# A paced top-k, an opening by passes, and three norm sums from fp32r halves in a two-block transformer kernel

## The chip, the cores and the metric

The kernel runs on one core of a Trainium2 chip. A core has a matrix engine (TensorE, PE in the profile; its weight load is PEld), a vector engine (VectorE, DVE), a scalar engine (ScalarE, ACT), GpSimd (POOL) and a sync engine (SyncE, SP), each with an instruction queue of its own; they wait for each other by semaphores. DMA queues bring data from memory, and all tiles live in on-chip memory (SBUF) or in the eight accumulator banks of PE (PSUM, "bank" in the profile). The metric is the device time of one execution in microseconds, lower is better.

## The reference, cut to what matters

Two transformer blocks run one after the other on 512 tokens of width 1024, all in float32.

```python
def first_block(x, ...):
    h = rmsnorm(x, ln1)                       # norm n1
    z = h @ w_in                              # pool, GLA and forgetting-attention (FoX) inputs
    mix = concat(y_pool, y_gla, y_fox)
    x = x + mix @ w_o
    h = rmsnorm(x, ln2)                       # norm n2
    gate, up = split(h @ w_gu)
    x = x + (silu(gate) * up) @ w_down
    return rmsnorm(x, ln_f)                   # norm n3 (its gain is folded on)

def second_block(x, ...):
    h = rmsnorm_2(x, norm_g)                  # norm n3f works on x as well
    q_lat, c_kv, k_rope, z_a, q_b, k_b, v_b, z_b, q_idx, k_idx, w_idx, gate_a, gate_b = split(h @ w_in)
    y_a = mla_attention(...) * silu(z_a)      # 8 heads, softmax over chunk-causal keys
    # index scores: relu(q_idx k_idx) weighted over 8 index heads; top 128 keys of each query
    _, idx = lax.top_k(score, 128)
    y_b = dsa_attention(... gathered by idx ...) * silu(z_b)
    merged = sigmoid(gate_a) * (y_a @ w_o_a) + sigmoid(gate_b) * (y_b @ w_o_b)
    return rmsnorm_2(x + merged @ w_out, final_g)
```

## The kernel before, in words

**Products.** Activations are held transposed: width on the 128 partitions, 512 tokens along the row. A dense product is made of 128x128 weight tiles, 1296 of them in all, in units of eight. Weights and activations are each split into a high and a low fp32r half, so that one tile costs three matmuls into the same bank: high x high (L1454), low activation (L1456) and low weight (L1458). `WS` holds a unit of weights as loaded, `WH` and `WL` its halves; ACT makes WH (L1638, 128x1024) and either DVE (L1856) or POOL (L2234, in quarters) makes WL. `HH` and `HL` are the halves of the activation x: ACT makes HH (L1646 in the opening, L1767 later), DVE HL (L1866, L2072).

**Order.** A planner in Python writes one list of steps with `do(...)`; each of the five engine programs walks that list and issues its part of each step. So the order on every engine is fixed when the program is built. A `product` yields after every two tiles; `weave(main, side, per)` runs the attention (`main`) and pulls steps of the side products (`side`) in between at a rate of `per`. `behind` is a list of lesser work. At every yield of a product `go_behind` adds `now["per"]` to a debt and issues one piece of that work for each whole unit of it. From the attention of the second block on, the list holds the top-k: `top(i)` gives 16 rounds for each of the query blocks i=3, 2, 1, and a round is one MAX8 (L2145) and one MATCH_REPLACE8 with its load (L2147) on DVE, 512 or 384 or 256 wide.

**Rings.** Banks and buffers are handed out by rings, each with the event that frees its next member: `d_ring` (banks 0, 1) for products, `s_ring` (2, 3) for logits, `t_ring` (4, 5) for turned shares and the sums, `y_ring` (6, 7) for attention outputs, `tmp_ring` (two 128x512 buffers) for temporaries of ACT and DVE.

**Attention.** For a unit (head pair, head, query block i) PE computes logits (L1562, L1563), DVE their row maximum (L2031), ACT the exponentials (L1736), DVE the inverse of the sum (RECIPROCAL, L2046), ACT multiplies (the share, L1741), PE turns the result by products with the identity (L1577), ACT moves it out of the bank (L1749) and PE mixes it with the values (L1586). I write (pair, n) for the n-th unit of a pair of MLA heads, counted through both heads, as in "the turn of unit (0,3)".

**Norms.** A norm needs the sum over the width of the squares. They are accumulated in a 128x512 fp32 tile `acc`; `column_sums` then does one fp32 product with a tile of ones (L1496, two records in the trace), and ACT computes exp(-0.5 ln(.)) of the bank (L1654, L1657) into `Rb` or `Rf`. There are six such sums: n1, n2, n3, n3f and those of the two latents of MLA. The sum of n2 stands after six of the eight tiles of the first gate product of the FFN (`gate0`), n3 inside the index query product `qi0`, n3f behind `qi1`; next on PE is there the latent product `ckv0`.

**The opening.** `start` issues on SP: vecs, the first half of the first weight unit (`WS[:, 0, 0:512]`), X chunk 0, its second half, X1, W1, X2, X3, W2 and so on. Until the first halves are ready PE runs 14 products of ones (28 records). Then the first three products (`firsts`: three columns of w_in) run together: for each chunk k of the input the three products have one tile each.

**The rope of the key** (`keys`, DVE L2122, L2123, L2125) takes both buffers of `tmp_ring` and gives them back when its last instruction ends; that is event `rope("end")`. It stands in the list right ahead of the sum of n3f (`norm_first`).

## Time and profile before

| | us |
|---|---|
| median of 3 runs | 1049.0 (1048.12 to 1049.06) |
| the profiled execution: its time | 1049.3 |
| its span in the trace | 1047.5 |
| PE busy | 1030.2 (98%) |
| PEld busy | 832.4 (79%) |
| DVE busy | 603.8 (58%) |
| ACT busy | 443.9 (42%) |
| POOL busy | 320.5 (31%) |
| granted clock of PE, mean | 0.997 |

The page gives busy time by engine, the span in 40 slices and the costliest groups of instructions. A timeline row gives the start, the duration, the engine and the instruction; in square brackets stands how long the engine was idle ahead of it and what ended that. Matmuls overlap in the records: a 128x512 fp32r matmul is drawn 0.39 us long, and the next begins 0.227 us after it (232.80, 233.02, 233.25 and so on in an undisturbed stretch), so the pace of PE is the distance of starts. What PE loses at a place is the distance of two starts less what that pair of instructions takes elsewhere, which is a little more than the idle time in brackets.

### The profile page before, as it was taken

The page shows a single profiled execution, that of the slowest core. Times are in us where ns is not written, and L with a number is a line of the kernel's source. Part 1 is how long each engine was busy: PE and PEld are TensorE (multiplying, and loading weights), DVE is VectorE, ACT ScalarE, POOL GpSimd, SP SyncE. Part 2 cuts the span into 40 slices and gives each one's busy share as a digit, 9 for nine tenths or more (in the row PEclk, how much of TensorE's full clock was granted, in tenths as well). Part 3 has the DMA queues.
Part 4 walks back from the last instruction along what each step waited for, and adds up shares of the span by engine and source line. Part 5 has one row for each costly group of instructions (what it writes and reads, how often), then busy time and mean ns, then how long its engine had stood idle before and what let it go on. Part 6 is the DMA issues. An engine that isn't in the chain of part 4 may idle for free.

```text
span 1047.5 us, 13717 instructions
## 1 busy us (share of the span) xinstructions
PE 1030.2 (98%) x5126; PEld 832.4 (79%) x5126; DVE 603.8 (58%) x1087; ACT 443.9 (42%) x785; POOL 320.5 (31%) x374
## 2 busy tenths in 40 slices
PE   9999999999999999999999999989999999999997
PEld 7887877778888888888888878767887777788886
DVE  5875657575444432444457657888656666335544
ACT  6432656554232221233242346445755554323233
POOL 1344632440110000110113347333336666521101
PEclk9999999999999999999999999999999999999999
DMA  8222233123323322323322335211322323222312
GB/s 287 92 71 86 82 91 94 62 77 104 100 84 104 115 92 90 101 81 101 101 101 89 126 115 190 81 61 45 98 67 85 116 88 109 84 98 95 106 61 81
DMA packets 34898, 102.39 MB, mean 98 GB/s; under 512 B 4608, under 2 KB 8128, under 8 KB 34832
## 3 DMA queue, kind: packets, MB, share of 16 engines
q1 hardware_dynamic: 34560, 101.25, 29.7%
q8 instruction: 41, 0.67, 0.3%
q10 hardware_dynamic: 272, 0.26, 0.1%
q14 instruction: 25, 0.20, 0.1%
HBM read 93.40 MB, written 4.74 MB: 94 GB/s over the span
## 4 chain that ended last, share of the span: by engine, by line
PE 85%; DVE 8%; ACT 3%; issue 2%; DMA 1%; POOL 0%; SPq 0%; DVEq 0%; ACTq 0%; POOLq 0%
PE bank L1454 23%; PE bank L1458 23%; PE bank L1456 23%; PE bank L1586 3%; PE bank L1577 2%; PE bank L1477 1%; DVE score L2147 1%; PE bank L1478 1%; PE bank L1479 1%; DVE m L2145 1%; PE bank L1562 1%; DVE acc L1875 1%; ACT WH L1638 1%; DMA X<-xT 1%; PE bank L1496 1%
## 5 line engine op out<-in xcount | busy, mean ns | idle before, releaser
L1454 PE MATMUL bank<-HH,WH 128*128 128x512 f32 x800 | 322.7, 403 | 0.9 <-DVE HL L1866 0.6
L1458 PE MATMUL bank<-HH,WL 128*128 128x512 f32 x800 | 312.9, 391 | 0.0
L1456 PE MATMUL bank<-HL,WH 128*128 128x512 f32 x800 | 312.5, 391 | 0.0
L2234 POOL TENSOR_TENSOR WL<-WS,WH 128x256 fp32r<-128x256 f32 x256 | 203.5, 795 | 255.6 <-ACT WH L1638 239.6
L1638 ACT ACTIVATE WH<-WS 128x1024 fp32r<-128x1024 f32 x160 | 166.3, 1047 | 41.6 <-PE bank L1458 40.2
L1454 PEld LDWEIGHTS bank<-HH,WH 128*128 128x128 f32 x800 | 151.0, 189 | 38.5 <-issue 5.8
L1458 PEld LDWEIGHTS bank<-HH,WL 128*128 128x128 f32 x800 | 150.4, 188 | 32.3
L1456 PEld LDWEIGHTS bank<-HL,WH 128*128 128x128 f32 x800 | 150.9, 189 | 29.4 <-issue 1.4
L1856 DVE TENSOR_TENSOR WL<-WS,WH 128x1024 fp32r<-128x1024 f32 x96 | 125.1, 1308 | 30.8 <-ACT WH L1638 30.8
L2275 POOL TENSOR_TENSOR fa<-fa,fg 128x512 f32<-128x512 f32 x22 | 28.3, 1286 | 271.6 <-DVE fa L2087 271.6
L1454 PE MATMUL bank<-GH,WH 128*128 128x512 f32 x176 | 68.5, 389 | 0.0
L1456 PE MATMUL bank<-GL,WH 128*128 128x512 f32 x176 | 68.5, 389 | 0.0
L1458 PE MATMUL bank<-GH,WL 128*128 128x512 f32 x176 | 68.5, 389 | 0.0
L2067 DVE TENSOR_TENSOR X<-X,bank 128x512 f32<-128x512 f32 x39 | 26.7, 685 | 66.5 <-PE bank L1458 66.4
L1775 ACT ACTIVATE GH<-fa 128x512 fp32r<-128x512 f32 x22 | 13.9, 632 | 114.6 <-POOL fa L2275 114.6
L1650 ACT ACTIVATE sq<-X 128x512 f32<-128x512 f32 x31 | 19.5, 629 | 75.4 <-DVE X L2067 75.3
L1477 PE MATMUL bank<-WH,HH 128*128 128x256 f32 x160 | 47.3, 296 | 0.1
L1749 ACT ACTIVATE PT<-bank 128x128 f32<-128x128 f32 (+1 forms) x96 | 41.1, 428 | 14.0 <-PE bank L1577 13.7
L1479 PE MATMUL bank<-WH,HL 128*128 128x256 f32 x160 | 45.2, 283 | 0.0
L1478 PE MATMUL bank<-WL,HH 128*128 128x256 f32 x160 | 45.2, 283 | 0.0
L2089 DVE TENSOR_TENSOR GL<-fa,GH 128x512 fp32r<-128x512 f32 x22 | 15.2, 692 | 47.1 <-ACT GH L1775 47.1
L1771 ACT ACTIVATE fs<-fg 128x512 f32<-128x512 f32 x22 | 13.9, 632 | 59.3 <-DVE fg L2078 59.3
(326 smaller groups left out, 1710.7 us busy)
## 6 DMA issues: line engine op xcount, KB each, us to landing
WS<-wall SPq DMA_DIRECT2D x161, 512.0 KB, 3.4
scratch<-rows SPq DMA_DIRECT2D x8, 320.0 KB, 5.4
X<-xT SPq DMA_DIRECT2D x8, 256.0 KB, 6.8
b_t<-scratch SPq DMA_DIRECT2D x8, 256.0 KB, 3.6
outT<-X SPq DMA_DIRECT2D x7, 256.0 KB, 2.3
b_m<-b_m SPq DMA_DIRECT2D x11, 128.0 KB, 2.3
f_s<-f_s SPq DMA_DIRECT2D x8, 128.0 KB
f_m<-f_m SPq DMA_DIRECT2D x8, 128.0 KB
```

What stands on the lines that cost most here:

```text
L1454: e.matmul(b[:, :], wh, xh[:, at_k, :], start=k == 0, stop=False)
L1456: e.matmul(b[:, :], wh, xl[:, at_k, :], start=False, stop=False)
L1458: m = e.matmul(b[:, :], wl, xh[:, at_k, :], start=False, stop=k == n - 1)
L1477: e.matmul(b[:, 0:256], xh[:, k, cs], wh, start=k == 0, stop=False)
L1478: e.matmul(b[:, 0:256], xh[:, k, cs], wl, start=False, stop=False)
L1479: m = e.matmul(b[:, 0:256], xl[:, k, cs], wh, start=False, stop=k == NK - 1)
L1586: m = e.matmul(b[64 * hl:64 * hl + 64, 128 * kb:512], v[:, kb, hd * 64:hd * 64 + 64], s["pt"][:, at_pt + 128 * kb:at_pt + 512], start=kb = ...
L1638: e.activation(WH[:, u % NW, :], WS[:, u % NST, :], ACT.Copy).then_inc(*w_hi.tick(u))
L1749: e.activation(dst, s["b"][:, 0:128 * i + 128].rearrange("p (a n) -> p a n", n=128), ACT.Copy).then_inc(*moved.tick(s["u"]))
L1856: e.tensor_tensor(WL[:, u % NW, :], WS[:, u % NST, :], f32(WH[:, u % NW, :]), ALU.subtract).then_inc(*w_low_v.tick(u))
L2234: e.tensor_tensor(WL[:, u % NW, cs], WS[:, u % NST, cs], f32(WH[:, u % NW, cs]), ALU.subtract).then_inc(*tick(w_low_g, u if c == 3 else (u ...
L2275: e.tensor_tensor(a[:, :], a[:, :], fg[jj % 3][:, :], ALU.mult).then_inc(*tick(gate_up, jj))
```

## The change

It has five parts.

1. **Opening.** X chunk 0 is issued by ACT, ahead of its table load, not by SP. On SP, X1 then stands in front of the second half of the first weights, X2 in front of W1, and X4 in front of W2. PE runs 10 products of ones, not 14. ACT and DVE halve the second part of the first weights after X1 rather than after X0. For each k, PE runs the three high products, then the three with the low activation, then the three with the low weight (`mm_firsts`).
2. **Sums from halves.** For n2, n3 and n3f ACT copies `acc` to an fp32r tile in one `tmp_ring` buffer (the high half), DVE subtracts it from `acc` into the other (the low half), and PE multiplies both with `ones_r`, two fp32r matmuls in the place of one fp32 matmul. POOL makes `ones_r` once.
3. **The place of n2.** The sum follows all eight tiles of `gate0`, not six.
4. **za1.** The gate product of MLA pair 1 (six tiles and two, 8 in all) opens the side products instead of following uq3; the first query product uq0 takes its bank from `t_ring`.
5. **Pacing.** `go_behind` no longer issues rounds (`now["per"]` is 0); `paced` wraps the attention and issues one round each time that .25 per attention step and .37 per product tile add up to 1. Ahead of `step_c` (the turn) of MLA there is one more yield to the side products.

```diff
@@ column_sums
+            halved = name in ("n2", "n3", "n3f")
+            if halved:
+                (m1, _, free1), (m2, _, free2) = tmp_ring.take(), tmp_ring.take()
+                do("sums_halves", name=name, a=a, ready=ready, hi=tmp_r[m1], lo=tmp_r[m2], free1=free1, free2=free2)
             i, b, free = t_ring.take()
-            do("sums", name=name, a=a, ready=ready, b=b, free=free)
+            if halved:
+                do("sums", name=name, halves=(tmp_r[m1], tmp_r[m2]), b=b, free=free)
+                tmp_ring.give(m1, sums(name))
+                tmp_ring.give(m2, sums(name))
+            else:
+                do("sums", name=name, a=a, halves=None, ready=ready, b=b, free=free)
@@ planner, the opening
-        do("split_first", half=0)
         for c in range(NK):
             do("halve_x", c=c)
-            if c == 0:
-                do("split_first", half=1)
+            if c < 2:
+                do("split_first", half=c)
...
-            for (name, _, _, _), (t, _), b in zip(firsts, tiles, early):
-                do("mm", name=name, tiles=[(t, k)], n=NK, x="h1", x0=0, b=b, free=None)
+            do("mm_firsts", names=[f[0] for f in firsts], tiles=[t for t, _ in tiles], k=k, b=early)
@@ the attention's order
                         if to_c:
+                            if to_c[0]["a"] == "mla":
+                                yield
                             step_c()
@@ gate_out, and the loop of the FFN
+                if jj == 0:
+                    ffn_norm()
                 do("ffn_gate", half=half, j=j, jj=jj, b=b)
...
-                if jj == 0:
-                    for _ in range(3):
-                        next(gen)
-                    ffn_norm()
@@ mla_products
-                                   + cols(96 * hd + 64, 16), "lq", 3, q_out(hd, hl))
-            if p:
+                                   + cols(96 * hd + 64, 16), "lq", 3, q_out(hd, hl),
+                                   ring=t_ring if hd == 0 else d_ring)
+            if p > 1:
                 yield from z_products("za", P_ZA, p)
...
         def mla_side():
+            yield from z_products("za", P_ZA, 1)
             yield from mla_products(1)
...
+        def paced(main, per_tile, per_step):
+            due, seen = 0.0, len(steps)
+            for _ in main:
+                yield
+                due += per_step + per_tile * sum(len(s["tiles"]) if kind == "mm" else 2 * (kind == "mm_tok")
+                                                 for kind, s in steps[seen:])
+                seen = len(steps)
+                while due >= 1:
+                    due -= 1
+                    step_behind()
...
-        now["per"] = 1.5
+        now["per"] = 0.0
@@ SP, the start
-                    for c in range(NK):
+                    for c in range(1, NK):
                         e.dma_start(X[:, c, :], xT[:, c, :]).then_inc(*x_in[c].tick())
-                        if c == 0:
+                        if c == 1:
                             e.dma_start(WS[:, 0, 512:1024], wall[0, :, 512:1024]).then_inc(*w_in[0].tick(0))
-                        elif c in (1, 3):
-                            load((c + 1) // 2)
+                        elif c in (2, 4):
+                            load(c // 2)
@@ PE
-                    for _ in range(14):
+                    for _ in range(10):
...
+                elif kind == "mm_firsts":
+                    k = s["k"]
+                    for t, b in zip(s["tiles"], s["b"]):
+                        q.wait_ge(hi(("h1", k)), w_hi("first" if t < 4 else t // UT))
+                        e.matmul(b[:, :], weights(t)[0], HH[:, k, :], start=k == 0, stop=False)
+                    for t, b in zip(s["tiles"], s["b"]):
+                        q.wait_ge(low(("h1", k)))
+                        e.matmul(b[:, :], weights(t)[0], HL[:, k, :], start=False, stop=False)
+                    for name, t, b in zip(s["names"], s["tiles"], s["b"]):
+                        q.wait_ge(w_low_v("first") if t < 4 else split_low(t // UT))
+                        m = e.matmul(b[:, :], weights(t)[1], HH[:, k, :], start=False, stop=k == NK - 1)
...
                 elif kind == "sums":
-                    q.wait_ge(s["ready"], s["free"], fill("ones"))
-                    e.matmul(s["b"][:, :], ones[:, :], s["a"][:, :], start=True, stop=True).then_inc(
-                        *sums.tick(s["name"]))
+                    if s["halves"]:
+                        hi_sum, lo_sum = s["halves"]
+                        q.wait_ge(norm_a(s["name"] + " hi"), s["free"], fill("ones_r"))
+                        e.matmul(s["b"][:, :], ones_r[:, :], hi_sum[:, :], start=True, stop=False)
+                        q.wait_ge(norm_v(s["name"] + " lo"))
+                        e.matmul(s["b"][:, :], ones_r[:, :], lo_sum[:, :], start=False, stop=True).then_inc(
+                            *sums.tick(s["name"]))
@@ ACT
+                    e.dma_start(X[:, 0, :], xT[:, 0, :]).then_inc(*x_in[0].tick())
                     e.preload_act_table_set(LN_EXP)
...
+                elif kind == "sums_halves":
+                    q.wait_ge(s["ready"], s["free1"])
+                    e.activation(s["hi"][:, :], s["a"][:, :], ACT.Copy).then_inc(*norm_a.tick(s["name"] + " hi"))
@@ DVE
+                elif kind == "sums_halves":
+                    q.wait_ge(norm_a(s["name"] + " hi"), s["free2"])
+                    e.tensor_tensor(s["lo"][:, :], s["a"][:, :], f32(s["hi"][:, :]), ALU.subtract).then_inc(
+                        *norm_v.tick(s["name"] + " lo"))
```

The opening on PE, before, from the products of ones on; the waits of a row stand in brackets by the name of the semaphore (hi and low: the halves of X; w_hi and w_low_v: those of the weights):

```order
L1443 MATMUL bank<-ones 128x128 x13
L1454 MATMUL bank<-HH,WH 128x512 [waits hi,w_hi]
L1456 MATMUL bank<-HL,WH 128x512 [waits low]
L1458 MATMUL bank<-HH,WL 128x512 [waits w_low_v]
L1454 MATMUL bank<-HH,WH 128x512
L1456 MATMUL bank<-HL,WH 128x512
L1458 MATMUL bank<-HH,WL 128x512
...
L1454 MATMUL bank<-HH,WH 128x512 [waits hi]
L1456 MATMUL bank<-HL,WH 128x512 [waits low]
L1458 MATMUL bank<-HH,WL 128x512
```

And now:

```order
L1468 MATMUL bank<-ones 128x128 x9
L1487 MATMUL bank<-HH,WH 128x512 [waits w_hi,hi]
L1487 MATMUL bank<-HH,WH 128x512 x2
L1490 MATMUL bank<-HL,WH 128x512 [waits low]
L1490 MATMUL bank<-HL,WH 128x512 x2
L1493 MATMUL bank<-HH,WL 128x512 [waits w_low_v]
L1493 MATMUL bank<-HH,WL 128x512 x2
L1487 MATMUL bank<-HH,WH 128x512 [waits hi]
L1487 MATMUL bank<-HH,WH 128x512 [waits w_hi]
L1487 MATMUL bank<-HH,WH 128x512
L1490 MATMUL bank<-HL,WH 128x512 [waits low]
```

What stood as a triple of high, low activation and low weight for each tile stands now as three passes, and each pass has the wait that it needs.

The sum of n3f on PE, before and now. The row ahead of it is the last tile of `qi1`, the one behind it the first of `ckv0`:

```order
L1458 MATMUL bank<-HH,WL 128x512
L1496 MATMUL bank<-acc_66,ones 128x512 [waits norm_a,total_g]
L1454 MATMUL bank<-HH,WH 128x512 [waits w_low_v,out_v]
L1456 MATMUL bank<-HL,WH 128x512
L1458 MATMUL bank<-HH,WL 128x512
```

```order
L1478 MATMUL bank<-HH,WL 128x512
L1533 MATMUL bank<-tmp_r,ones_r 128x512 [waits norm_a]
L1535 MATMUL bank<-tmp_r,ones_r 128x512 [waits norm_v]
L1476 MATMUL bank<-HH,WH 128x512 [waits w_low_v,out_v]
L1477 MATMUL bank<-HL,WH 128x512
L1478 MATMUL bank<-HH,WL 128x512
```

ACT around the same place, before and now (L1697 is the copy into the high half, L1842 the halves of the index queries, L1701 and L1704 the norm, L1682 the weight splits):

```order
L1638 ACTIVATE WH<-WS 128x1024 [waits dense,w_in2]
L1790 ACTIVATE i_kk<-i_s 32x512 [waits out_v]
L1791 ACTIVATE i_kk<-i_s 32x512
L1795 ACTIVATE i_qh<-i_q 128x512 [waits out_v] x2
L1654 ACTIVATE Rf<-bank,eps 128x512 [waits sums]
L1657 ACTIVATE Rf<-Rf 128x512 [waits norm_a]
L1638 ACTIVATE WH<-WS 128x1024 [waits dense,w_in0]
L1638 ACTIVATE WH<-WS 128x1024 [waits dense,w_in1]
```

```order
L1682 ACTIVATE WH<-WS 128x1024 [waits dense,w_in2]
L1837 ACTIVATE i_kk<-i_s 32x512 [waits out_v]
L1838 ACTIVATE i_kk<-i_s 32x512
L1842 ACTIVATE i_qh<-i_q 128x512 [waits out_v] x2
L1697 ACTIVATE tmp_r<-acc_67 128x512 [waits rope,total_g]
L1701 ACTIVATE Rf<-bank,eps 128x512 [waits sums]
L1704 ACTIVATE Rf<-Rf 128x512 [waits norm_a]
L1682 ACTIVATE WH<-WS 128x1024 [waits dense,w_in0]
```

DVE there, now: the rope of the key takes L2173 to L2176, and L1925 makes the low half:

```order
L2168 TENSOR_TENSOR i_ql<-i_q,i_qh 128x512 [waits istack_a] x2
L2173 TENSOR_TENSOR tmp_72<-i_s,RT 32x512 [waits sums,rope_in,out_v]
L2174 TENSOR_TENSOR tmp_71<-i_s,RT 32x512
L2176 TENSOR_TENSOR a_k_199<-tmp_72,tmp_71 32x512 [waits rope]
L1925 TENSOR_TENSOR tmp_r<-acc_67,tmp_r 128x512 [waits rope,norm_a]
```

The sum waits for `norm_a` (the copy) and `norm_v` (the subtraction), where it waited for the total; the copy waits for `rope` as well, which is the end of the row L2176 of DVE. On ACT the copy stands in front of the two weight splits.

DVE from the RECIPROCAL (the inverse sum) of the MLA unit (0,1) to that of (0,3), before (L2145 and L2147 are a round of the top-k, L1891 and L1895 the gate product za1):

```order
L2046 RECIPROCAL small<-small 128x1 [waits exps]
...
L2145 MAX m_74<-score 128x8 [waits topk]
L2147 MATCH_REPLACE score<-m_74,score 128x512 [waits topk]
L2145 MAX m_74<-score 128x8 [waits topk]
L2147 MATCH_REPLACE score<-m_74,score 128x512 [waits topk]
L2145 MAX m_74<-score 128x8 [waits topk]
L2147 MATCH_REPLACE score<-m_74,score 128x512 [waits topk]
L2046 RECIPROCAL small<-small 128x1 [waits exps]
...
L1891 SCALAR_TENSOR_TENSOR zb_212<-bank,Rb 128x512 [waits dense]
L1895 SCALAR_TENSOR_TENSOR zb_212<-tmp_71,zb_212 128x512 [waits tanh]
L2145 MAX m_74<-score 128x8 [waits topk]
...
L2046 RECIPROCAL small<-small 128x1 [waits exps]
```

And now (rounds are L2196 and L2198, L2223 writes the queries of the next pair):

```order
L2097 RECIPROCAL small<-small 128x1 [waits exps]
L2082 TENSOR_REDUCE small<-bank 128x1 [waits share_v,logits]
L2223 SCALAR_TENSOR_TENSOR a_q_197<-bank,RQ 128x512 [waits dense]
L2196 MAX m_77<-score 128x8 [waits topk]
L2198 MATCH_REPLACE score<-m_77,score 128x512 [waits topk]
L2097 RECIPROCAL small<-small 128x1 [waits exps]
L2082 TENSOR_REDUCE small<-bank 128x1 [waits share_v,logits]
L2223 SCALAR_TENSOR_TENSOR a_q_198<-bank,RQ 128x512 [waits dense]
L2196 MAX m_77<-score 128x8 [waits topk]
L2198 MATCH_REPLACE score<-m_77,score 128x512 [waits topk]
L2196 MAX m_77<-score 128x8 [waits topk]
...
L2097 RECIPROCAL small<-small 128x1 [waits exps]
```

Five rounds and the gate (za1) stood between the two in the order before; three rounds and the queries of the next pair stand there now. Ahead of the RECIPROCAL of (0,3) there were nine rounds in all, now there are six.

## Rows read from the trace of the kernel before

**Rows 1.** The page: busy times, and the chain that ended last.

```profile
PE 1030.2 (98%) x5126; PEld 832.4 (79%) x5126; DVE 603.8 (58%) x1087; ACT 443.9 (42%) x785; POOL 320.5 (31%) x374
...
PE 85%; DVE 8%; ACT 3%; issue 2%; DMA 1%; POOL 0%; SPq 0%; DVEq 0%; ACTq 0%; POOLq 0%
```

**Rows 2.** PE's timeline, 0 to 16 us (start, length, instruction, [idle before]).

```profile
1.00 5.98 PE L1443 MATMUL bank<-ones 128*128 128x128 f32 x28 [1.00 <-POOL ones L2215]
...
14.26 0.50 PE L1454 MATMUL bank<-HH,WH 128*128 128x512 f32 x1 [0.31 <-DVE HL L1866]
```

**Rows 3.** The same timeline, ACT and then DVE.

```profile
10.01 0.72 ACT L1646 ACTIVATE HH<-X,V 128x512 fp32r<-128x512 f32 x1 [1.15 <-DMA X<-xT]
10.64 1.04 ACT L1638 ACTIVATE WH<-WS 128x1024 fp32r<-128x1024 f32 x1
...
13.46 0.75 DVE L1866 SCALAR_TENSOR_TENSOR HL<-X,V,HH 128x512 fp32r<-128x512 f32 x1
```

**Rows 4.** Timeline, 233 to 240 us (the sum of n2): PE, ACT, DVE.

```profile
234.73 1.12 PE L1496 MATMUL bank<-acc,ones 128*128 128x512 f32 x2 [0.41 <-DVE acc L1875]
...
235.93 0.40 PE L1456 MATMUL bank<-HL,WH 128*128 128x512 f32 x1
...
234.47 1.04 ACT L1638 ACTIVATE WH<-WS 128x1024 fp32r<-128x1024 f32 x1
...
234.60 0.75 DVE L2072 SCALAR_TENSOR_TENSOR HL<-X,V,HH 128x512 fp32r<-128x512 f32 x1
235.54 1.23 DVE L1856 TENSOR_TENSOR WL<-WS,WH 128x1024 fp32r<-128x1024 f32 x1 [0.19 <-ACT WH L1638]
```

**Rows 5.** Groups of instructions of the page: busy us, mean ns of one.

```profile
L1775 ACT ACTIVATE GH<-fa 128x512 fp32r<-128x512 f32 x22 | 13.9, 632 | 114.6 <-POOL fa L2275 114.6
...
L2089 DVE TENSOR_TENSOR GL<-fa,GH 128x512 fp32r<-128x512 f32 x22 | 15.2, 692 | 47.1 <-ACT GH L1775 47.1
```

**Rows 6.** Timeline, 593 to 599 us (the sum of n3): DVE, PE.

```profile
594.29 3.44 DVE L1856 TENSOR_TENSOR WL<-WS,WH 128x1024 fp32r<-128x1024 f32 x2
...
597.50 1.02 PE L1496 MATMUL bank<-acc,ones 128*128 128x512 f32 x2
...
598.60 0.40 PE L1456 MATMUL bank<-HL,WH 128*128 128x512 f32 x1
```

**Rows 7.** Timeline, 606 to 617 us (the sum of n3f): PE, DVE.

```profile
607.93 1.02 PE L1496 MATMUL bank<-acc,ones 128*128 128x512 f32 x2
...
609.21 0.39 PE L1456 MATMUL bank<-HL,WH 128*128 128x512 f32 x1
...
609.57 1.29 DVE L2117 TENSOR_TENSOR i_ql<-i_q,i_qh 128x512 fp32r<-128x512 f32 x2
...
612.33 1.11 DVE L2125 TENSOR_TENSOR a_k<-tmp,tmp 32x512 f32<-32x512 f32 x1
```

**Rows 8.** PE at 685 us, and a stretch: length, PE busy, PEclk 0.50.

```profile
685.37 0.84 PE L1577 MATMUL bank<-ident,Pc 128*128 128x128 f32 x4 [2.73 <-ACT Pc L1741]
...
685.70:689.10 3.40, 3.40 (x11) 2.63 (x9) 3.30 (x9) 1.72 (x5) 0.00 (x0) 0.50 0.45 159
```

**Rows 9.** Ten us of the attention: length, then busy PE, PEld, DVE.

```profile
665.00:675.00 10.00, 10.00 (x47) 7.73 (x46) 9.70 (x24) 3.54 (x10) 3.18 (x6) 1.00 0.20 72
```

**Rows 10.** Timeline of PE, 657 to 727 us: the other waits.

```profile
660.36 0.50 PE L1454 MATMUL bank<-LQH,WH 128*128 128x512 f32 x1 [1.09 <-DVE a_k L2169]
...
704.29 0.65 PE L1586 MATMUL bank<-PT,a_v 128*64 128x512 f32 x2 [0.41 <-ACT PT L1749]
...
724.38 0.44 PE L1577 MATMUL bank<-ident,Pc 128*128 128x128 f32 x2 [0.97 <-ACT Pc L1741]
```

**Rows 11.** Timeline of DVE, 680 to 709 us.

```profile
680.89 0.69 DVE L1895 SCALAR_TENSOR_TENSOR zb<-tmp,zb 128x512 f32<-128x512 f32 x1 [1.04 <-ACT tmp L1660]
...
684.41 0.15 DVE L2046 RECIPROCAL small<-small 128x1 f32<-128x1 f32 x1
...
707.65 0.69 DVE L2172 SCALAR_TENSOR_TENSOR a_q<-bank,RQ 128x512 f32<-128x512 f32 x1 [2.12 <-PE bank L1458]
```

27 lines of the change are left out of this document (17 added, 10 removed).

## The prediction

> **What bounds the kernel now.** Read the busy times first [rows 1]: PE is busy for 1030.2 of 1047.5 us, and the chain that ended last runs over PE for 85% of the span. So a faster ACT, DVE or POOL is worth nothing in itself. What can be won are the places where PE stands still, the products of ones ahead of the first real one, and the fp32 sums. What can be lost is any new place where PE must wait. I therefore went through PE's timeline for rows in which the distance of two starts is more than the usual 0.227 us, and then read the timelines of ACT and DVE at each of these places, to see which instruction is the late one and what stands ahead of it. The largest lot, 7.9 us, lies between 660 and 727 us, in the MLA attention. Its worst row is the turn of unit (0,3), with 2.73 us of idle [rows 8].
>
> The sum is made against the profiled execution (1049.3 us). The median is 0.3 lower, and the changes are taken over to it unaltered.
>
> **Opening: -1.35 us.** PE waits last at 14.26 us, for the low half of X3 [rows 2]. From there on it runs without a gap. So what counts is when HL3 is ready and how much of the work of k=3 is done by then. HL3 is made at 13.46 to 14.21; its engine was held up by the weight split, that waits for ACT's WH at 10.64, which stood behind HH2, for which ACT waited 1.15 us for the DMA of X2 [rows 3]. With X2 issued ahead of the weights, HH2 comes earlier; W1 now lands behind X2, an estimate of 10.0 us since the two together end where X2 ended before (10.01). WH then starts at 10.0 instead of 10.64, so everything behind it is 0.65 earlier. Then the passes: three high products of k=3, 3 x 0.227 = 0.68 us, need only HH3 and run inside the wait. Together 1.35. The cover is that PE, with fewer waits, doesn't meet HL4 or the next WL late; HL4 follows HL3 on DVE by an addition and itself, some 1.4 us [rows 3, 5], and a k costs PE 9 x 0.227 = 2.05 us, so it doesn't. Bounds: -0.7 (the passes alone) to -2.0 (a further wait, at 11.57 [rows 2], goes as well). The products of ones took 5.98 us for 14, so ten end near 5.3, before PE is fed; that costs nothing unless the clock comes later (below).
>
> **n2: +0.65 us.** Before, the sum stood after six tiles at 234.73, and the second matmul of the next tile at 235.93, 1.20 us later, where a plain one is 0.227 later [rows 4]. Two short matmuls would take 0.45, so 0.5 is to be won where nothing waits. But now all eight tiles come first, and the last one waits for HL7 (234.60 + 0.75 = 235.35) [rows 4]. The copy stands on ACT behind the WH split (to 235.51) and takes 0.63 [rows 4, 5], so to 236.15. The subtraction (0.69 [rows 5]) stands on DVE behind the WL split, which ends at 236.77 [rows 4]: ready 237.46. The short pair follows, and the first product of `up0` starts at about 237.75, not 237.09 (the six matmuls from 235.93 less one, at 0.227). That is +0.65; between +0.2 (the subtraction slips ahead) and +0.9. The norm `Rb` comes later too, but the bank of `gate0` is wanted only six us on, so that hides.
>
> **n3: +0.33 us.** The sum cost 598.60 - 597.50 = 1.10, less 0.227. Now the subtraction stands on DVE behind two WL splits that end at 594.29 + 3.44 = 597.73 [rows 6], so it is ready at 598.42; the next tile starts at 598.70, not 598.37. Between 0 and +0.5.
>
> **n3f: +7.7 us, the term that decides.** Before, this sum took `acc` as it was: 607.93, and the tile behind it was under way by 609.21 [rows 7], at pace from 608.98. Now the copy needs both buffers of `tmp_ring`, and these are held by the rope of the key, which comes one step before it in the list. The copy's row says so: it waits for `rope`. On DVE the rope is the last of a row of work: the index queries' low halves at 609.57 (two of them), then three instructions of 32x512, the last from 612.33 to 613.44 [rows 7]. None of it waits for PE any longer, and none gets faster, save that last instruction: it took 1.11 us beside a WL split on POOL that won't have begun, where a plain one takes 0.69 [rows 5], so it may end at 613.0. Copy 0.63, subtraction 0.69 [rows 5], with some 0.1 for the signals: 614.4 to 614.9. Behind the two short matmuls `ckv0` starts at 614.7 to 615.2 instead of 608.98: +5.7, between +5.5 and +6.2. Behind the waiting matmul on PE's queue stands all of the rest; behind the waiting copy on ACT stand the norm and two weight splits, which come some 5 us later than before; their units are wanted on PE over 10 us after the wait, so that hides. Then the clock: after the idle of 2.73 us at 682.6 PE had clock 0.50 for 3.4 us, and its matmuls came every 0.43 us [rows 8], so some 1.6 us were lost; waits of 1.09 and 0.97 us [rows 10] cost none. A wait of over five us is past the 2.73 that did it; I take 2.0, between 1.5 and 2.7. The sum is 7.7.
>
> A rule of the Trainium skill stands behind the purpose of this part. FP8 and Floating Point Precision, section TensorE Precision Notes, says that a true fp32 product takes four passes through the array. The rows agree (about 0.9 for the sum and 0.227 for an fp32r matmul). By that rule alone the three sums would give back some 1.5 us together, where I have +8.7 from the waits.
>
> **MLA attention: -4.4 us.** What PE loses here before, each as the distance of starts beyond the pace: 1.5 at 660.36, where uq1 waits for the bank of uk0 [rows 10], 2.9 at 685.37 and 1.6 by the clock behind it [rows 8], 1.14 at 724.38, 0.35 at 704.29 [rows 10] and 0.38 in one place more: 7.9 in all. The first goes, since uq0 takes its bank from another ring and six tiles of za1 stand in front, less 0.3 for the next wait of that kind. The second is the turn of unit (0,3): its RECIPROCAL is late, at 684.41, behind a wait of DVE for the gate za1 (1.04 us at 680.89) and nine rounds [rows 11] of about 1.5 us (two of them fill the time from the gate's end, 681.5, to 684.41). In the new order six rounds stand there, and the gate is done long before. But PE comes earlier too: DVE is busy for 9.70 of 10 us [rows 9], so what it has less to do ahead of that unit, PE doesn't find waiting for it. I count the share ready at 682.4 and PE there at 681.3: 1.1 is left. And the rounds that are not ahead of (0,3) are ahead of a later one. In the old order DVE had caught up at 705 us (2.12 us of idle at 707.65 [rows 11]); with PE over 4 us earlier it has not, and the turn of (2,2) waits 2.05 by my count (ready 708.85, PE 706.8). So 7.9 - 0.3 - 1.1 - 2.05 = 4.4. Bounds: 3 (the wait of 2 us costs clock as well) to 6.5 (rounds are spread well enough for one of the two to hide).
>
> A rule of the skill bears on DVE here. SBUF, section on the two separate sides, says that a DVE instruction with two SBUF inputs and a GpSimd instruction that reads SBUF exclude one another. This trace agrees: 3.44 us for two WL splits beside POOL [rows 6], 1.23 for one [rows 4]. Where the rounds move beside POOL's splits, DVE could lose more than I count; no row here has a price for the rounds.
>
> **Sum.** -1.35 + 0.65 + 0.33 + 7.7 - 4.4 = +2.9, so 1051.9 us.
>
> **The rivals.**
> - *The attention gives back nearly all.* If the paced rounds remove all 7.9 and the opening 2.0, with the rest as above: 1049.0 - 7.9 - 2.0 + 8.7 = 1047.8. For it speaks that rounds come one at a time and each unit has some slack; against it DVE's 9.70 of 10 [rows 9], for pacing moves work on DVE and takes none away. 0.22.
> - *DVE is the bound and the pacing gives nothing.* Each us won at (0,3) is lost at the next turn; only the 1.5 of the start stays: 1049.0 - 1.35 + 8.7 - 1.5 = 1054.9. 0.15.
> - *The other side: the n3f sum does not hold PE.* If the copy finds its buffers free, or the rope ends long before 613, the three sums cost +0.5 in all: 1049.0 - 1.35 + 0.5 - 4.4 = 1043.7. It decides for faster from the point where n3f costs under 2.6 us, clock included; `ckv0` starts 1.7 after the rope's end, so the rope would have to be over by 609.9, which [rows 7] speak against. The copy's row names `rope`, so 0.06.
> - *The clock.* The fall of the clock comes twice more, behind the 2 us wait at (2,2) and in the opening with its shorter warm-up, at 1.6 each [rows 8]: 1051.9 + 3.2 = 1055.1. Against it, waits of 1.09 and 0.97 cost nothing [rows 10]. 0.12.
> - The forecast, each term within its bounds: 0.45, from 1050.2 to 1053.6.
>
> **How the numbers follow.** This kernel's runs differ by about 0.1%; 0.2%, 2.1 us, is what can be told from no change. Faster (under 1046.9): the rope rival and a quarter of the first, 0.12. Same (to 1051.1): three quarters of the first and a quarter of the forecast's own range, 0.28. Slower: 0.60. The range takes in most of each case but the one on the rope: 1046.8 to 1055.2.
>
> **What would show it.** In the trace after, PE's row of the first short sum matmul of n3f has an idle of over 5 us in brackets, put down to ACT or DVE, and PEclk shows 0.50 behind it; the copy on ACT starts where the rope's last instruction ends. The opening's last wait of PE stands before 14 us and is shorter, and PE's sum of n1 comes 1.3 earlier. `up0` starts 2 us after HL7 is done. In the attention the turn of (0,3) waits about 1 us at full clock, and that of (2,2) about 2. The prediction is wrong if the n3f row has no such idle, if DVE shows idle time between 665 and 705, or if the clock falls in the opening.

## The result, and the profile after

| | before | changed |
|---|---|---|
| median | 1049.01 us (12 runs, 1047.92 to 1049.36) | 1051.68 us (12 runs, 1050.33 to 1052.56) |
| ratio of the changed kernel to the one before | | 1.0026, 95% interval 1.0019 to 1.0034 |
| the profiled execution: time, span | 1049.3, 1047.5 | 1051.26, 1049.4 |
| granted clock of PE, mean | 0.997 | 0.994 |

The changed kernel is slower by 0.26%: 2.7 us by the medians, 1.96 by the two profiled executions. The page of the changed kernel (compare [rows 1]):

```profile
PE 1028.1 (98%) x5118; PEld 831.6 (79%) x5118; DVE 604.2 (58%) x1090; ACT 445.8 (42%) x788; POOL 319.3 (30%) x375
```

PE is busy 2.1 us less in a span that is 1.9 us longer, so PE stands still for 4 us more. As before, the time is made of the places where it waits. I compare the two timelines of PE at points that both kernels pass in the same order:

| PE reaches | before | changed | difference | of this part |
|---|---|---|---|---|
| the sum of n1 | 22.55 | 20.63 | -1.92 | opening -1.92 |
| the first tile of `up0`, behind n2 | 237.09 | 235.89 | -1.20 | n2 +0.72 |
| the last matmul of `qi1`, behind n3 | 607.70 | 606.86 | -0.84 | n3 +0.36 |
| the sum of the first latent | 628.35 | 635.08 | +6.73 | n3f +7.57 |
| the last mix of the attention (L1586, L1629) | 902.28 | 904.13 | +1.85 | attention -4.88 |
| its last instruction | 1040.29 | 1042.15 | +1.86 | 0 |

**Opening.** ACT, then DVE, then PE; L1690 is ACT's HH, L1682 its WH, L1913 DVE's HL (compare [rows 2, 3]):

```profile
8.17 0.71 ACT L1690 ACTIVATE HH<-X,V 128x512 fp32r<-128x512 f32 x1
9.35 1.06 ACT L1682 ACTIVATE WH<-WS 128x1024 fp32r<-128x1024 f32 x1 [0.47 <-DMA WS<-wall]
...
12.19 0.74 DVE L1913 SCALAR_TENSOR_TENSOR HL<-X,V,HH 128x512 fp32r<-128x512 f32 x1
...
12.19 0.84 PE L1487 MATMUL bank<-HH,WH 128*128 128x512 f32 x3
12.99 0.97 PE L1490 MATMUL bank<-HL,WH 128*128 128x512 f32 x3
```

HH2 starts at 8.17, where it was 10.01, and WH1 at 9.35, where it was 10.64. HL3 is at 12.19 instead of 13.46. PE's waits at 11.57 and 14.26 are gone; its passes follow each other with only some 0.25 us lost between 12.19 and 13.80, where two passes of three matmuls take 0.80 and 0.81 instead of 0.68. The figure of -1.92 is that of one pair of executions. In the runs below the sum of n1 stands between 22.13 and 23.54 us with the old opening and between 19.95 and 21.14 with the new one, so the medians of the runs are the better measure of this part.

**n2.** PE and DVE (compare [rows 4]):

```profile
233.53 0.50 PE L1476 MATMUL bank<-HH,WH 128*128 128x512 f32 x1 [0.41 <-DVE HL L2123]
...
234.33 0.40 PE L1533 MATMUL bank<-tmp_r,ones_r 128*128 128x512 f32 x1
235.55 0.50 PE L1535 MATMUL bank<-tmp_r,ones_r 128*128 128x512 f32 x1 [0.82 <-DVE tmp_r L1925]
...
233.66 1.23 DVE L1903 TENSOR_TENSOR WL<-WS,WH 128x1024 fp32r<-128x1024 f32 x1 [0.19 <-ACT WH L1682]
234.81 0.69 DVE L1925 TENSOR_TENSOR tmp_r<-acc,tmp_r 128x512 fp32r<-128x512 f32 x1
```

The eighth tile waits 0.41 us for HL7, and the second short matmul 0.82 us for the subtraction, which stands behind the weight split at 233.66. `up0` begins at 235.89, 1.56 us after the first short matmul.

**n3** (compare [rows 6]):

```profile
597.20 0.50 PE L1535 MATMUL bank<-tmp_r,ones_r 128*128 128x512 f32 x1 [0.50 <-DVE tmp_r L1925]
...
593.09 3.45 DVE L1903 TENSOR_TENSOR WL<-WS,WH 128x1024 fp32r<-128x1024 f32 x2
596.47 0.68 DVE L1925 TENSOR_TENSOR tmp_r<-acc,tmp_r 128x512 fp32r<-128x512 f32 x1
```

The same with two weight splits, 0.50 us of wait.

**n3f.** PE, ACT, DVE (compare [rows 7, 8]):

```profile
606.86 0.39 PE L1478 MATMUL bank<-HH,WL 128*128 128x512 f32 x1
612.95 0.80 PE L1533 MATMUL bank<-tmp_r,ones_r 128*128 128x512 f32 x1 [5.70 <-ACT tmp_r L1697]
613.67 0.80 PE L1535 MATMUL bank<-tmp_r,ones_r 128*128 128x512 f32 x1
...
612.26 0.63 ACT L1697 ACTIVATE tmp_r<-acc 128x512 fp32r<-128x512 f32 x1 [3.62 <-DVE a_k L2176]
...
611.49 0.68 DVE L2176 TENSOR_TENSOR a_k<-tmp,tmp 32x512 f32<-32x512 f32 x1
612.92 0.69 DVE L1925 TENSOR_TENSOR tmp_r<-acc,tmp_r 128x512 fp32r<-128x512 f32 x1 [0.76 <-ACT tmp_r L1697]
```

And by stretches (length, busy PE, PEld, DVE, ACT, POOL, then PEclk, DMA):

```profile
612.90:617.25 4.35, 4.30 (x9) 3.10 (x10) 1.63 (x9) 2.71 (x4) 0.31 (x1) 0.50 0.30 79
```

The rope's last instruction runs from 611.49 to 612.17, the copy starts at 612.26, PE after 5.70 us of idle at 612.95, the subtraction is ready at 613.61. From 612.90 to 617.25 PE has half its clock.

**Attention.** PE's waits between 655 and 730 us, then one row of DVE (compare [rows 9 to 11]):

```profile
679.74 0.50 PE L1476 MATMUL bank<-LQH,WH 128*128 128x512 f32 x1 [0.87 <-DVE a_k L2220]
...
683.38 0.44 PE L1620 MATMUL bank<-ident,Pc 128*128 128x128 f32 x2 [0.33 <-ACT Pc L1788]
684.02 0.50 PE L1476 MATMUL bank<-HH,WH 128*128 128x512 f32 x1 [0.21 <-DVE a_q L2223]
...
690.40 0.66 PE L1620 MATMUL bank<-ident,Pc 128*128 128x128 f32 x4 [0.75 <-ACT Pc L1788]
...
708.67 2.37 PE L1629 MATMUL bank<-PT,a_v 128*64 128x512 f32 x16 [0.72 <-ACT PT L1796]
...
715.99 0.55 PE L1620 MATMUL bank<-ident,Pc 128*128 128x128 f32 x3 [0.44 <-ACT Pc L1788]
...
677.67 0.69 DVE L1946 SCALAR_TENSOR_TENSOR zb<-tmp,zb 128x512 f32<-128x512 f32 x1 [1.15 <-ACT tmp L1707]
```

And by stretches (length, busy PE, PEld, DVE, ACT, POOL, then PEclk, DMA):

```profile
665.00:675.00 10.00, 10.00 (x49) 8.27 (x48) 7.38 (x13) 3.54 (x8) 6.39 (x8) 1.00 0.24 80
...
685.00:695.00 10.00, 9.25 (x47) 7.07 (x47) 9.79 (x26) 5.41 (x13) 2.94 (x4) 1.00 0.15 55
```

The waits of 2.73 and 1.09 us and the fall of the clock behind the first are gone, and so is that of 0.97; the mix that waited 0.41 now waits 0.72. In their place stand six short ones, 3.3 us of idle in all and 4.5 by the distances of starts, at full clock. That is 3.4 less than the 7.9 of the prediction, and not the whole of the 4.88. The kernel before had one more wait further on, which the prediction didn't list, at a turn of the second attention (DSA):

```profile
841.34 0.55 PE L1577 MATMUL bank<-ident,Pc 128*128 128x128 f32 x3 [0.55 <-DVE Pc L2049]
```

It cost 0.73 by the distance of starts and is gone; a new one of 0.37 stands at 822.59. Some 1.1 us of the gain I can assign to no single row. DVE was busy 9.70 of the ten us from 665; now it is 7.38, and then 9.79 from 685. PE comes to this place 6.7 us later than before, but that is not why DVE has idle time there: from 672 to 682 it is busy for 6.89.

Two names have to be put right here. The change's part 5 calls `step_c` the turn; in the kernel `step_b` issues the turn and `step_c` the mix, so the further yield puts dense work in front of the mix. And the unit that the prediction calls (2,2) is in the second pair, pair 1 if the first is 0: the wait at 715.99 is the turn of (1,2), and the one at 724.38 before was that of (1,5).

### The profile page after: what moved, and what is told of

It is laid out like the page before. It is cut to its first block, busy times and chain, and to the rows that moved or that the text cites. A ratio compares the mean times of both kernels' runs of the same rounds, so it can differ in the third digit from the quotient of the medians.

```text
span 1049.4 us, 13707 instructions
## 1 busy us (share of the span) xinstructions
PE 1028.1 (98%) x5118; PEld 831.6 (79%) x5118; DVE 604.2 (58%) x1090; ACT 445.8 (42%) x788; POOL 319.3 (30%) x375
## 4 chain that ended last, share of the span: by engine, by line
PE 85%; DVE 10%; ACT 3%; issue 2%; DVEq 0%; POOL 0%; ACTq 0%; POOLq 0%
PE bank L1476 23%; PE bank L1478 23%; PE bank L1477 23%; PE bank L1629 2%; PE bank L1620 2%; DVE score L2198 1%; PE bank L1512 1%; PE bank L1514 1%; PE bank L1513 1%; DVE m L2196 1%; PE bank L1605 1%; ACT WH L1682 1%; DVE X L2118 1%; DVE acc L1922 1%; PE bank L1487 1%
## 5 line engine op out<-in xcount | busy, mean ns | idle before, releaser
L1476 PE MATMUL bank<-HH,WH 128*128 128x512 f32 x776 | 312.1, 402 | 0.9 <-DVE HL L2123 0.4
L1478 PE MATMUL bank<-HH,WL 128*128 128x512 f32 x776 | 303.5, 391 | 0.0
L1477 PE MATMUL bank<-HL,WH 128*128 128x512 f32 x776 | 303.1, 391 | 0.0
L1682 ACT ACTIVATE WH<-WS 128x1024 fp32r<-128x1024 f32 x160 | 166.3, 1047 | 42.9 <-PE bank L1478 40.2
L1476 PEld LDWEIGHTS bank<-HH,WH 128*128 128x128 f32 x776 | 146.6, 189 | 34.2 <-issue 3.6
L1478 PEld LDWEIGHTS bank<-HH,WL 128*128 128x128 f32 x776 | 145.9, 188 | 31.4
L1477 PEld LDWEIGHTS bank<-HL,WH 128*128 128x128 f32 x776 | 146.5, 189 | 28.3 <-issue 1.0
```

Of the source, the lines that this page charges most:

```text
L1476: e.matmul(b[:, :], wh, xh[:, at_k, :], start=k == 0, stop=False)
L1477: e.matmul(b[:, :], wh, xl[:, at_k, :], start=False, stop=False)
L1478: m = e.matmul(b[:, :], wl, xh[:, at_k, :], start=False, stop=k == n - 1)
L1682: e.activation(WH[:, u % NW, :], WS[:, u % NST, :], ACT.Copy).then_inc(*w_hi.tick(u))
```

## The experiments

The twelve ran in three groups, each beside the kernel before on the same chip: the four `n3f_fp32`, `n3f_early`, `n3f_own_buffers` and `n3f_busy` (before: 1049.23 us) on one chip, then `n3f_sum_early`, `open_only`, `open_14_ones` and `attn_only` (1048.90) and the last four (1049.00) on another. The interval of a ratio is about 0.09% to each side with 11 runs and 0.13% with 5, so 0.9 to 1.4 us; smaller differences between two medians are read in the traces only.

### Is it the n3f sum? One product again

```diff
-            halved = name in ("n2", "n3", "n3f")
+            halved = name in ("n2", "n3")
```

> The changed kernel, with the sum of n3f alone as one fp32 product again. Theory (the n3f sum cost 7.6 us, 5.9 of wait and 1.7 of clock): 1051.7 - 7.6 = 1044.1 us, and no stretch with granted clock 0.50 between 600 and 630 us. Rival (the wait of PE at n3f only took the place of a wait that comes later anyway, in the latents or the MLA attention): most of it is paid again, 1049 or more.

Measured: 1043.42 us (5 runs, 1043.02 to 1043.80), ratio to the kernel before 0.9943 (0.993 to 0.9955). From the sum of n3 to that of the first latent PE needs 31.19 us, where the changed kernel needs 38.77: 7.58 less, and from there to the last instruction both need 407.07. So the whole cost sits at this place, and nothing of it was only put off. The clock is 1.00 from 5 us to the end of the last product.

### Buffers or place: own buffers for the halves

```diff
-                (m1, _, free1), (m2, _, free2) = tmp_ring.take(), tmp_ring.take()
-                do("sums_halves", name=name, a=a, ready=ready, hi=tmp_r[m1], lo=tmp_r[m2], free1=free1, free2=free2)
+                if name == "n3f":
+                    hi_sum, lo_sum = own_sum
+                    do("sums_halves", name=name, a=a, ready=ready, hi=hi_sum, lo=lo_sum, free1=None, free2=None)
...
```

> The changed kernel, with two buffers of its own for the halves of n3f (32 KB into the area where the low halves of the latents stand later), so that the copy on ACT doesn't wait for the rope; the order is unchanged. Theory A, as the prediction put it (the buffers held by the rope make the wait): the wait goes, 1044. Theory B (the place on DVE's queue: the subtraction stands behind the rope whatever buffers it has): the copy starts at 608.7 instead of 612.3, the subtraction at 612.2 instead of 612.9, so only 0.7 to 0.8 us are won, 1050.9, and PE's long idle is then in front of the second short matmul.

Measured: 1050.87 us (11 runs), ratio 1.0013 (1.0004 to 1.0022), 0.8 under the changed kernel by the medians, which is within the interval. PE, ACT (the copy), DVE (the subtraction):

```profile
609.03 0.50 PE L1540 MATMUL bank<-own_sum,ones_r 128*128 128x512 f32 x1 [1.97 <-ACT own_sum L1704]
612.76 0.80 PE L1542 MATMUL bank<-own_sum,ones_r 128*128 128x512 f32 x1 [3.23 <-DVE own_sum L1932]
...
608.36 0.61 ACT L1704 ACTIVATE own_sum<-acc 128x512 fp32r<-128x512 f32 x1
...
612.01 0.69 DVE L1932 TENSOR_TENSOR own_sum<-acc,own_sum 128x512 fp32r<-128x512 f32 x1
```

The copy is made at 608.36, 3.9 us earlier, and PE takes it. But the subtraction still runs at 612.01, since on DVE it stands behind the rope. PE's one wait is cut in two, of 1.97 and 3.23 us, and the clock falls as before. From the sum of n1 to that of the first latent it is 614.21 us where the changed kernel needs 614.45, so the trace shows a gain of only 0.2. The second short matmul starts 0.74 us earlier, counted from the sum of n1, but more of the work behind it is done at clock 0.50. Theory B holds: what the rope holds back is DVE's queue, and the buffers come second.

### The place in the list

First the whole norm of n3f was put ahead of the outputs of the index products:

```diff
         def norm_first():
-            norm("n3f", acc[0], total_g(("n3f", 7)), Rf, D)
             token_norm("n3t", "n3", Rb, 0)
...
+        norm("n3f", acc[0], total_g(("n3f", 7)), Rf, D)
         for out in later:
             out()
```

> The changed kernel, with the norm of n3f ahead of the outputs of the index products in the list of steps, so ahead of the rope of the key; the token norm stays where it was. The halves of n3f are made as in the changed kernel. Theory (the sum is late only for the place of its two halves in the list, behind the rope): copy and subtraction are done by 600 us, PE meets both short matmuls ready, no idle, 7.6 + 0.5 (two short matmuls for one fp32) less than the changed kernel: 1043.6 us. Rival (halves are dear in themselves, wherever they stand, since ACT and DVE have no room beside the weight splits): 2 us or more of wait stay at the sum, 1046 or more.

Measured: 1049.56 us (11 runs), ratio 1.0004 (0.9995 to 1.0013). Neither theory gave this. PE takes both short matmuls at 607.04 without any wait and is 7.6 us earlier at the first latent; from there to the end it needs 6.2 us more than the changed kernel. PE, ACT, and the DMA issues of SP (SPq):

```profile
637.93 0.44 PE L1647 MATMUL bank<-i_kk,i_qq 96*128 96x384 f32 x1 [1.55 <-ACT i_t L1850]
...
635.21 1.06 ACT L1682 ACTIVATE WH<-WS 128x1024 fp32r<-128x1024 f32 x1 [5.27 <-DMA WS<-wall]
...
610.91 0.58 SPq L1421 DMA_DIRECT2D i_qq<-i_qh  x1
...
630.57 1.08 SPq L1351 DMA_DIRECT2D WS<-wall  x2
```

And SP in the changed kernel, the first issue for the index stack and the first load of weights behind it:

```profile
603.90 0.58 SPq L1421 DMA_DIRECT2D i_qq<-i_qh  x1
...
623.94 1.08 SPq L1351 DMA_DIRECT2D WS<-wall  x2
```

The step `norm` brought the logarithm and exponential of ACT along, and these wait for PE's sum at 607.7. The halves of the index keys, which ACT makes from 601.93 in the changed kernel, come behind them, at 608.97. SP waits for the halves; behind that wait stand 24 issues for the index queries of 0.63 us each, then seven more, and only then the loads of weights. The first issue goes out at 610.91 instead of 603.90 and the weights at 630.57 instead of 623.94. ACT waits 5.27 us for them at 635.21, and its queue is then late with the index scores, for which PE waits 1.55 us at 637.93. At 655.90 PE waits 1.91 us more, for DVE to empty a bank; on DVE's queue the index scores stand ahead of that (two of them from 653.17 to 655.25). After this second wait the clock falls.

So the next kernel moves the halves and the sum alone:

```diff
         def norm_first():
-            norm("n3f", acc[0], total_g(("n3f", 7)), Rf, D)
+            i, b = n3f_sum
+            do("norm", name="n3f", r=Rf, n=D, b=b, bias=eps[:, 0:1])
+            t_ring.give(i, norm_a("n3f ln"))
...
+        n3f_sum = column_sums("n3f", acc[0], total_g(("n3f", 7)))
         for out in later:
             out()
```

> The changed kernel, with the halves and the sum of n3f ahead of the outputs of the index products in the list, but its logarithm and exponential on ACT where they were, behind the halves of the index keys and queries (the run before moved them in front of these, and PE then waited 1.71 us at 636 and 2.47 us at 653, at the index scores and behind them). Theory (all of the cost of n3f, and of the run before too, is the order of steps): no wait at the sum and none at the index scores, 1043.4 - 0.5 = 1042.9 us. Rival (with the buffers of the rope taken for the halves earlier, the rope or the index stack is late again): 1045 or more.

Measured: 1043.58 us (5 runs, 1043.05 to 1043.72), ratio 0.9946 (0.9932 to 0.9959). All of the cost is gone with the halves kept. It is the order of the steps. But against one fp32 product (1043.42) nothing is won. PE:

```profile
607.04 0.40 PE L1536 MATMUL bank<-tmp_r,ones_r 128*128 128x512 f32 x1
607.28 0.40 PE L1538 MATMUL bank<-tmp_r,ones_r 128*128 128x512 f32 x1
607.99 0.50 PE L1479 MATMUL bank<-HH,WH 128*128 128x512 f32 x1 [0.31 <-DVE i_q L1945]
```

The two short matmuls take 0.45 us instead of the 0.94 from 607.20 to 608.14 in the kernel with one fp32 product, and then PE waits 0.31 us for DVE to empty the bank of `qi1`. The long product had stood in that time: from the sum of n3f to that of the first latent it is 20.41 us with the fp32 product and 20.43 with the halves.

### What the clock takes

```diff
                         hi_sum, lo_sum = s["halves"]
+                        if s["name"] == "n3f":
+                            q.wait_ge(s["free"])
+                            for _ in range(25):
+                                e.matmul(s["b"][:, 0:128], ones[:, :], ones[:, :], start=True, stop=True)
```

> The changed kernel, with 25 products of ones (128x128, fp32, into the bank of the sum) on PE ahead of its wait at n3f, 5.5 us of work at full clock that is thrown away. It costs nothing as long as it ends before 612.9. Theory (1.7 us of the cost of n3f come from the clock, which falls because PE stands idle): the clock stays at 1.00, 1050.0 us. Rival (the clock costs less, or the first matmuls behind a wait are slow anyway): within 0.5 us of the changed kernel.

Measured: 1049.40 us (11 runs), ratio 1.0000 (0.9991 to 1.0009), 2.3 under the changed kernel by the medians. PE, and the stretch that had been at half clock:

```profile
606.37 5.74 PE L1535 MATMUL bank<-ones 128*128 128x128 f32 x50
612.23 0.50 PE L1537 MATMUL bank<-tmp_r,ones_r 128*128 128x512 f32 x1
612.95 0.50 PE L1539 MATMUL bank<-tmp_r,ones_r 128*128 128x512 f32 x1 [0.23 <-DVE tmp_r L1929]
```

And by stretches (length, busy PE, PEld, DVE, ACT, POOL, then PEclk, DMA):

```profile
612.90:617.25 4.35, 4.30 (x19) 3.55 (x20) 0.94 (x8) 3.22 (x4) 1.24 (x2) 1.00 0.30 79
```

The same wait, with PE at work on products of ones: the clock stays at 1.00, and the matmuls behind come every 0.23 us. From the sum of n1 to that of the first latent it is 612.72 us in place of 614.45, so 1.73 us by the trace (1.72 to the last instruction). The medians show 0.6 more, which is within their interval and which I leave open.

### The opening

The opening alone (steps of the opening as in the diff ahead of the prediction, nothing else):

> The kernel before, with the opening of the change alone (X0 issued by ACT, the order of SP, 10 products of ones, halves of the weights by X1, three passes). Theory (the trace: the n1 sum at 20.6 instead of 22.55 us, and the gain is kept to the end): 1049.0 - 1.9 = 1047.1 us. Rival (a part of it is lost again in the first block, where PE waits for weights or the n1 norm): 1048 or more.

Measured: 1047.17 us (11 runs), ratio 0.9981 (0.9973 to 0.9990). With 14 products of ones:

```diff
-                    for _ in range(10):
+                    for _ in range(14):
```

> The same, with the 14 products of ones of the kernel before. The prediction took their number for worth nothing and the order of the weights and the passes for all of the gain. Theory A (the prediction): no difference to 10, 1047.1. Theory B (in the new opening PE meets nearly no wait behind its first product, so what counts is when that one starts; 14 products end at 7.0, ten at 5.6 us): PE starts 1.1 to 1.4 us later, of which at most the 0.1 of wait that is left comes back, 1048.2 to 1048.4.

Measured: 1047.38 us (11 runs), ratio 0.9984 (0.9976 to 0.9993). The number of ones makes no difference that can be told in the time, as the prediction had it, but two effects stand behind that. PE's first products with ten ones, then with 14:

```profile
5.65 1.54 PE L1460 MATMUL bank<-HH,WH 128*128 128x512 f32 x3
...
6.72 0.95 PE L1460 MATMUL bank<-HH,WH 128*128 128x512 f32 x3
```

With ten they start 1.07 us earlier, but their starts, and that of the next pass, are 0.56, 0.43 and 0.39 us apart, where they are 0.32, 0.24 and 0.23 apart with 14. At clock 0.50 behind n3f a matmul of this size took 0.43 us, so I read this as PE still at half its clock until about 7.0 us (the trace's first record of clock 1.00 is at 6.98, with 14 at 6.43). By the sum of n1 the lead of 1.07 us has shrunk to 0.48. With the order alone (X0 by ACT, SP's order, the halves of the weights by X1), and triples and 14 ones as before:

> The kernel before, with the order of the opening alone (X0 by ACT, SP's order, halves of the weights by X1), the triples and the 14 products of ones as before. The prediction gave 0.65 us of the opening to the order and 0.68 to the passes; both together measured 1.5 to 1.7. Theory (the terms of the prediction): 1049.0 - 0.7 = 1048.3 us. Rival (the passes are nearly all of it: with triples PE now waits for the low half of the second weights at its second tile): 1049.0 or slower.

Measured: 1047.60 us (11 runs), ratio 0.9987 (0.9978 to 0.9996). ACT and PE:

```profile
8.09 0.71 ACT L1646 ACTIVATE HH<-X,V 128x512 fp32r<-128x512 f32 x1
8.95 1.06 ACT L1638 ACTIVATE WH<-WS 128x1024 fp32r<-128x1024 f32 x1
...
6.38 0.47 PE L1453 MATMUL bank<-HH,WH 128*128 128x512 f32 x1
```

Most of the gain is the order's: 1.4 of 1.7 us. WH1 starts at 8.95, 1.7 us earlier than before [rows 3], and PE shows no wait at all behind its first triple. So the passes find nothing to fill; what is left for them is 0.2 to 0.4 us, which the interval doesn't separate from nothing. In the traces the sum of n1 stands at 20.87 with the order alone, at 20.66 with the passes and ten ones and at 21.14 with the passes and 14, so with 14 ones in both the passes come out behind. The opening of the changed kernel gives between 19.95 and 20.76 from one execution to the next, so none of these differences says anything for or against the passes.

### The attention

Its parts alone, on the kernel before:

> The kernel before, with the attention's parts of the change alone (za1 first, uq0 in the other ring, paced top-k, one yield more ahead of the turn). Theory (the trace: 4.9 us between the last latent sum and the last turns, without any tie to the other parts): 1049.0 - 4.9 = 1044.1 us. Rival (DVE meets PE in another phase without the delay of 7.6 us at n3f): 1045.5 or more.

Measured: 1044.18 us (5 runs), ratio 0.9954 (0.9942 to 0.9967), 4.7 less than the kernel before beside it, and 4.88 less by its trace: 245.79 us from the last latent sum to the last mix, where it was 250.67 before and 245.79 in the changed kernel. The delay at n3f plays no part in it. Then each half:

```diff
+                            if to_c[0]["a"] == "mla":
+                                yield
...
-        now["per"] = 1.5
+        now["per"] = 0.0
...
+        weave(paced(attention(...), .37, .25), side, [0.9] * 66 + [0.85])
```

> The kernel before, with the paced top-k and the further yield ahead of the turn alone; za1 and the bank of uq0 as before. Theory (the two parts of the attention's gain add up: 3.4 us from the rounds, 1.3 from the start): 1049.0 - 3.4 = 1045.6 us, with the wait of 1.09 us for uq1's bank still there and no clock of 0.50 at 685 us. Rival (the gain is that of the rounds alone, and za1 at the start only swaps one wait for another): 1044.5.

Measured: 1043.33 us (5 runs, 1043.20 to 1044.08), ratio 0.9946 (0.9934 to 0.9959). That is 5.7 under the kernel before and 0.85 under both halves together, which the two intervals don't tell apart; 245.07 us by the same two points, 0.71 less than with both. PE's waits between 655 and 730 us:

```profile
660.01 0.50 PE L1468 MATMUL bank<-LQH,WH 128*128 128x512 f32 x1 [1.09 <-DVE a_k L2183]
...
707.43 0.55 PE L1591 MATMUL bank<-ident,Pc 128*128 128x128 f32 x3 [0.42 <-ACT Pc L1755]
...
727.94 2.27 PE L1600 MATMUL bank<-PT,a_v 128*64 128x512 f32 x14 [0.67 <-ACT PT L1763]
```

And by stretches (length, busy PE, PEld, DVE, ACT, POOL, then PEclk, DMA):

```profile
675.00:685.00 10.00, 10.00 (x52) 7.97 (x51) 8.76 (x21) 5.71 (x14) 3.05 (x4) 1.00 0.31 98
```

The wait of 1.09 for uq1's bank is there as before. None of the turns of the first pair waits, and what is left behind it are 0.42 us at the turn of (1,2) and 0.67 at a mix. DVE is not less loaded for it: from 685 to 695 it is busy for 9.77 of ten us and PE waits 0.15. What has changed is when the instruction comes that PE waits for. Six rounds stand ahead of the RECIPROCAL of (0,3), as in the changed kernel, where there were nine, and counted from the last latent sum it starts after 29.5 us, where it was 32.8 before and is 31.1 with both halves. The further yield ahead of the mix came in with the pacing, and which of the two wins was not run. And the other half:

```diff
-                                   + cols(96 * hd + 64, 16), "lq", 3, q_out(hd, hl))
-            if p:
+                                   + cols(96 * hd + 64, 16), "lq", 3, q_out(hd, hl),
+                                   ring=t_ring if hd == 0 else d_ring)
+            if p > 1:
                 yield from z_products("za", P_ZA, p)
...
+            yield from z_products("za", P_ZA, 1)
             yield from mla_products(1)
```

> The kernel before, with za1 at the head of the side products and uq0 in the other ring alone; the rounds come as before, 1.5 to each yield of a product. Theory (adds up): 1049.0 - 1.3 = 1047.7 us. Rival A (DVE is the bound as long as the rounds come so early: PE arrives sooner and waits longer, at the turns of (0,2) or (0,3)): 1049.0. Rival B (the gate away from in front of (0,3) is what removes the long wait and the fall of the clock, not the pacing): 1045.5.

Measured: 1049.12 us (11 runs), ratio 1.0000 (0.9991 to 1.0009). Nothing is won that the medians show (0.27 us by the same two points of the trace), as rival A had it, though the wait is at another place. PE, then DVE (L1893 empties the bank of za1):

```profile
672.41 0.50 PE L1456 MATMUL bank<-LQH,WH 128*128 128x512 f32 x1 [2.26 <-DVE zb L1893]
...
686.66 0.66 PE L1579 MATMUL bank<-ident,Pc 128*128 128x128 f32 x4 [0.75 <-ACT Pc L1743]
...
671.67 0.68 DVE L1893 SCALAR_TENSOR_TENSOR zb<-bank,Rb 128x512 f32<-128x512 f32 x1
```

With za1 at the start, its output on DVE stands behind four rounds in a row (they fill DVE from 665.59 to 671.48), and the product that wants its bank waits 2.26 us; the clock is 0.50 for 3.4 us behind it. The turn of (0,3) waits only 0.75 us, where it was 2.73 before. But its RECIPROCAL is no earlier: nine rounds still stand ahead of it, and it starts 33.2 us after the last latent sum, where it was 32.8. PE has done its waiting already. So the waits of 1.09 and 2.73 us were swapped for those of 2.26 and 0.75 and one of 0.63 at 698.98, with one fall of the clock as before, and rival B (the gate in front of (0,3) makes the wait) fails.

### Both parts that win, without the halves

The opening and the attention as changed, all sums in fp32:

> The opening and the attention of the change, on the kernel before, with all sums in fp32 and that of n2 after six tiles as before. Theory (the parts add up: -1.8 and -4.8): 1042.4 us, one us under the changed kernel with n3f alone in fp32 (1043.4), which is then the cost of the halves at n2 and n3 (predicted 0.65 + 0.33). Rival (n2's and n3's halves cost nothing on the whole): 1043.4.

Measured: 1042.61 us (5 runs, 1042.19 to 1043.09), ratio 0.9938 (0.9926 to 0.9951): 6.4 us under the kernel before and 9.1 under the changed one, the best that was run. It is 0.8 under the changed kernel with n3f in fp32, and 1.1 by the two traces from the sum of n1 on, which is the halves of n2 and n3 together with the place of n2; the ratios (0.9938 and 0.9943) don't tell the two kernels apart. The halves and the place of n2 were not run apart. Nor was the opening with the pacing alone, without za1 and uq0's ring; an estimate from the parts (1042.61 less the 0.85 above) puts it near 1041.8.

## Why the prediction was right, point by point

The forecast was 1051.9 us, the measurement 1051.68. That the two agree to 0.2 us is luck. By the trace the five terms were off by -0.57, +0.07, +0.03, -0.13 and -0.48, so they add up to +1.85 where the forecast had +2.9, and the medians happen to lie 0.7 further apart than the two profiled executions.

**Opening, -1.35 forecast, -1.92 in the trace, -1.7 measured alone.** The direction and the chain over WH1 and HL3 were right, and so was the claim that the number of ones makes no difference in the time. The term was mis-sized in one step: W1 was taken to land at 10.0, since the two transfers together would end where X2 had ended before. They ended 0.65 us earlier. By the landings in the traces X2 came at 9.98 before, behind W1 at 9.31; now X2 comes at 7.71 and W1 at 9.33. One thing that the estimate left out, and that no run moved alone, is that X0 is issued on ACT's queue at 0.76 us, where it went out on SP's at 1.65, so that it lands at 4.10 instead of 5.19. WH1 came 1.29 earlier, not 0.64, and HL3 at 12.19. That took away both of PE's waits (the bound of -2.0), and with them the ground of the second term: the 0.68 us of the passes were to be won inside a wait that wasn't there any more. The run with the order alone shows it.

**n2, +0.65 forecast, +0.72.** By the steps given: HL7, then the subtraction behind the weight split. **n3, +0.33 forecast, +0.36.** Together 1.08 in the trace, 0.8 by the medians of two kernels. The Trainium skill says that a true fp32 product takes four passes (FP8 and Floating Point Precision, TensorE Precision Notes); by an estimate from that rule each sum should have saved some 0.5. The trace agrees in that the short matmuls are that much shorter (0.45 for the pair instead of 0.94), and the runs show where the saving goes: into waits for the halves, or, with the halves ready, into one for the next bank.

**n3f, +7.7 forecast, +7.57; 7.58 with it taken back.** The wait was 5.86 by the distance of starts (forecast 5.7), the clock 1.73 (forecast 2.0). The timing was right since the rope's end fixes both ways. The reason was put too narrowly: the prediction named the buffers that the rope holds. Own buffers won 0.2 us by the trace, 0.8 by the medians; the subtraction stands behind the rope on DVE in any case. It was said in the working that the subtraction comes after the rope and the copy, but not that it would do so with free buffers. The last instruction of the rope took 0.68, not 1.11, as was allowed for.

**Attention, -4.4 forecast, -4.88.** The sum was right and its parts were not. The turn of (0,3) lost 0.91 (1.1 was forecast), and the second one that the prediction counted, (1,2), lost 0.61 (2.05 forecast). But four waits stood where at most 0.3 was put: 1.11 and 0.45 at products that want the banks of the next pair's keys and queries, 0.50 at the turn of (0,1), and 0.88 at the mix at 708.67. The first comes from za1: DVE waits 1.15 us for ACT's tanh at 677.67, and the keys of the next pair are behind it. The step that failed is the gain of 1.5 less 0.3 from za1 and uq0. Alone that part won next to nothing (0.27 by the trace), and with the pacing it cost 0.7 by the trace; the pacing, with its further yield, won 5.6 alone. "Pacing moves work on DVE and takes none away" was true and beside the point: DVE's 9.70 of 10 us was a matter of 1.5 rounds for each yield. Spread out it is 8.76 in the ten us shown above and 9.77 in the ten behind them, and no turn of the first pair waits. So the busy share of DVE didn't tell how long PE waits; the place of the one instruction that PE waits for did. The worry that the rounds get longer beside POOL's splits didn't come true: at 128x512 MAX8 takes 0.68 to 0.70 us in both kernels. At the places that the prediction looked at, 3.4 us were won, not 4.4. That the sum came out right is luck: it got 0.4 from the wait at 841.34, which was missed, less the new one at 822.59, and 1.1 from small differences that I can't place.

**The rivals.** "The n3f sum does not hold PE" was wrong as a description of this kernel, and right as a price: moved ahead, the sum costs nothing, and the time falls to 1043.6, where 1043.7 was put. The condition that the prediction gave for it, that the copy finds its buffers free, is not enough: with that alone the time is 1050.87. "DVE is the bound and pacing gives nothing" fell with the run of the pacing alone. Between the first products and the last the clock fell once, at n3f, and not in the opening nor at the turn of (1,2), whose wait was 0.44 us.

**The signs.** Those for n3f all came: an idle of 5.70 us, the clock at 0.50, the copy 0.09 us behind the rope's last instruction. The sum of n1 came 1.9 us earlier, not 1.3, and `up0` started 2.4 us behind HL7. But one sign by which the prediction called itself wrong came too, idle time of DVE between 665 and 705 us: it was busy for 7.38 of the first ten and 8.58 of the next. The picture of a DVE that is full throughout, which gave the 2.05 us at the second turn, did not hold there, and waits that were not foreseen stood in its place.

## What to carry to other kernels

A step that is split into pieces on several engines is as late as its last piece's place in the most loaded queue, so look up what stands ahead of each piece in each queue, and compute the whole of the short version's chain before the saving on the bound engine is counted. Moving a step moves its instructions on every engine: the norm that was moved whole held ACT, through ACT the issues of SP, and through these the weights, 28 us further on. Lesser work that is spread evenly over a loaded engine was worth more here than any single step moved out of its way, and two edits that each shorten the same stretch should be run apart before they are kept together.

## What the runs showed of the hardware

- PE's clock fell from 2.4 to 1.2 GHz (1.00 to 0.50 in the profile) with idles of 5.70 us, of 1.97 and 3.23 us with one matmul between, of 2.73 us in the kernel before, of 2.26 and of 1.91 us; it stayed up through idles of 0.97, 1.09 and 1.55 us. With 25 products of ones in an idle of 5.9 us it stayed at 1.00, and that was worth 1.73 us.
- A DMA issue on SP's queue for a row set of the index queries took 0.63 us; 31 issues in a row hold the queue for 20 us, and a load of weights behind them is that late.
- A transfer issued ahead of another did not make that one late here: with X2 in front of W1, and X0 on ACT's queue instead of SP's, HH2 could start 1.84 us earlier (8.17 for 10.01), and W1 landed at 9.33, where it was 9.31.
- A weight split of 128x1024 on DVE beside an addition on POOL took 2.31 us, and the next one, with POOL idle, 1.21 (the kernel before, from 594.29 us).
